# The 64 small transfers of the last attention are begun by GpSimd instead of SyncE

## The reference

```python
def first_block(x, ...):                 # gated linear attention + dilated attention, then a gated FFN
    x = x + mix @ w_out
    x = x + (silu(h2 @ w_gate) * (h2 @ w_up)) @ w_down

def second_block(x, ...):
    x = x + even_mixer(rms_norm_2(x), ...)   # retention and a short convolution
    x = x + odd_mixer(rms_norm_2(x), ...)    # the last attention

def odd_mixer(h, w_in, q_norm_w, k_norm_w, sinks, w_out, pos):
    q, k, v, gate = split(h @ w_in)          # 32 query heads, 4 key/value heads, 64 wide
    q = rope(rms_norm_2(q, q_norm_w), pos)
    k = rope(rms_norm_2(k, k_norm_w), pos)
    o = swa_sinks(q, k, v, sinks)            # softmax in a window of 128 tokens, with a sink per head
    return (o * silu(gate)) @ w_out
```

## Time and profile before

| | us |
|---|---|
| median of three runs (1873.78 to 1875.99) | 1874.39 |
| the profiled execution | 1875.87 |
| its span, first to last instruction | 1874.0 |
| TensorE busy in the span (99%) | 1862.7 |
| VectorE busy (66%) | 1246.1 |
| ScalarE busy (54%) | 1002.7 |
| GpSimd busy (2%) | 35.8 |

### The profile page before, as it was taken

How to read it: one execution, slowest core, us unless ns; L and a number is a source line. 1 busy time by engine, 2 the same in 40 slices (tenths; PEclk the granted TensorE clock), 3 DMA queues, 4 the chain that set the end, 5 groups by cost and what they waited for, 6 DMA issues and landing times.

```text
span 1874.0 us, 22288 instructions
## 1 busy us (share of the span) xinstructions
PE 1862.7 (99%) x8403; PEld 1534.2 (82%) x8403; DVE 1246.1 (66%) x1833; ACT 1002.7 (54%) x1422; POOL 35.8 (2%) x90
## 2 busy tenths in 40 slices
PE   9999999999999999999999999999999999999999
PEld 7888888888888888888888888888888888877777
DVE  6676566776666556665466776765676666776786
ACT  6677554554444344443444455564565545476763
POOL 0001000000000000000000000000000001001100
PEclk9999999999999999999999999999999999999999
DMA  9667764786666666666666686666666678677985
GB/s 324 202 194 179 207 183 151 215 257 192 195 193 193 193 191 191 193 197 196 189 198 194 201 281 203 192 191 190 185 203 198 193 238 241 202 234 216 268 255 174
DMA packets 223628, 388.36 MB, mean 207 GB/s; under 512 B 15696, under 2 KB 45184, under 8 KB 223520
## 3 DMA queue, kind: packets, MB, share of 16 engines
q1 hardware_dynamic: 222272, 384.17, 68.3%
q0 software_dynamic: 816, 2.11, 0.8%
q10 hardware_dynamic: 432, 0.66, 0.1%
HBM read 367.83 MB, written 19.05 MB: 206 GB/s over the span
## 4 chain that ended last, share of the span: by engine, by line
PE 95%; DMA 2%; DVE 1%; ACT 1%; SPq 0%; issue 0%; DVEq 0%; ACTq 0%
PE g L1341 31%; PE g L1342 30%; PE g L1343 30%; DMA PTB<-probs 1%; DMA queries<-TWQ 1%; DVE wl L1797 1%; PE ob L1404 1%; ACT wh L1513 0%; DMA queries<-TE 0%; DMA probs<-A 0%; PE m L1391 0%; PE m L1483 0%; DMA A<-queries 0%; PE m L1283 0%; DVE TWQ L1797 0%
## 5 line engine op out<-in xcount | busy, mean ns | idle before, releaser
L1797 DVE TENSOR_TENSOR wl<-raw,wh 128x1024 fp32r<-128x1024 f32 (+1 forms) x660 | 802.0, 1216 | 554.1 <-ACT wh L1513 551.0
L1513 ACT ACTIVATE wh<-raw 128x1024 fp32r<-128x1024 f32 (+1 forms) x661 | 695.2, 1053 | 750.2 <-PE g L1343 739.5
L1341 PE MATMUL g<-wh,xh 128*128 128x512 f32 x1886 | 740.7, 393 | 0.0
L1343 PE MATMUL g<-wh,xl 128*128 128x512 f32 x1886 | 735.6, 390 | 0.0
L1342 PE MATMUL g<-wl,xh 128*128 128x512 f32 x1886 | 735.6, 390 | 0.0
L1341 PEld LDWEIGHTS g<-wh,xh 128*128 128x128 f32 x1886 | 354.5, 188 | 78.4 <-issue 3.8
L1343 PEld LDWEIGHTS g<-wh,xl 128*128 128x128 f32 x1886 | 354.5, 188 | 74.1
L1342 PEld LDWEIGHTS g<-wl,xh 128*128 128x128 f32 x1886 | 354.6, 188 | 72.2
L1341 PE MATMUL g<-wh,mh 128*128 128x512 f32 x732 | 287.6, 393 | 0.4 <-issue 0.4
L1343 PE MATMUL g<-wh,ml 128*128 128x512 f32 x732 | 285.4, 390 | 0.0
L1342 PE MATMUL g<-wl,mh 128*128 128x512 f32 x732 | 285.3, 390 | 0.0
(11 more groups left out here) (175 smaller groups left out, 716.3 us busy)
## 6 DMA issues: line engine op xcount, KB each, us to landing
raw<-in_ev_w_in SPq DMA_DIRECT2D x128, 512.0 KB, 3.8
raw<-in_w_in SPq DMA_DIRECT2D x92, 512.0 KB, 4.4
raw<-in_w_gate SPq DMA_DIRECT2D x88, 512.0 KB, 4.4
raw<-in_w_up SPq DMA_DIRECT2D x88, 512.0 KB, 4.4
raw<-in_w_down SPq DMA_DIRECT2D x88, 512.0 KB, 4.8
raw<-in_od_w_in SPq DMA_DIRECT2D x72, 512.0 KB, 4.5
raw<-in_w_out SPq DMA_DIRECT2D x32, 512.0 KB, 4.2
raw<-in_ev_w_out SPq DMA_DIRECT2D x32, 512.0 KB, 4.8
```

The lines of the kernel that those rows point to most:

```text
L1341: e.matmul(o, hi[:, kt, c], h, start=first, stop=False)
L1343: last = e.matmul(o, lo[:, kt, c], h, start=False, stop=end)
L1513: return e.activation(o, i, AF.Copy, scale=scale)
L1797: return e.tensor_tensor(o, a, b, op)
```

## The change

SyncE no longer begins `qsend`, `qfetch`, `psend` and `pfetch`: the same 64 instructions with the same waits now stand in GpSimd's list, in the order of the plan. The plan's rules change with it: `on_root` is placed when the query fetch should have landed (so GpSimd's list has room for other transfers ahead of it), the assumed durations are 6 and 6.5 us for probabilities out and back (6.5 and 8.5 before) and 6.5 for the query fetch (7), `on_sum` is held until the transfer that reads its buffer has ended by 1.5 us, and VectorE may have a backlog of 4 us instead of 3 in the attention and 6 instead of 4.5 ahead of `mmul`. No computation changes.

```diff
@@ after(), queries @@
                     for i in range(2):
+                        while a[0] and self.end[("qsend", a[0] - 1, i)] + 1.5 > self.now:
+                            yield 1
                         say("on_sum", a[0], i)
@@ queries_back @@
             self.say("qfetch", j)
-            self.end[("qfetch", j)] = self.now + 7
-            yield 2
+            self.end[("qfetch", j)] = self.now + 6.5
+            while self.end[("qfetch", j)] > self.now:
+                yield 1
             self.say("on_root", j)
@@ probs_back @@
-        self.end[("psend", g)] = self.now + 6.5
+        self.end[("psend", g)] = self.now + 6
...
-        self.end[("pfetch", g)] = self.now + 8.5
+        self.end[("pfetch", g)] = self.now + 6.5
@@ fetched @@
-            yield from self.room("dve", 4.5)
+            yield from self.room("dve", 6)
             self.say("mmul", p[4])
@@ od_quad, five places @@
-            yield from self.room("dve", 3)
+            yield from self.room("dve", 4)
@@ gpsimd(): these four branches are taken out of sync() and stand here unchanged @@
+                elif kind == "qsend":
...
+                    e.dma_start(queries_there[k], queries_own[k]).then_inc(s_qsend[k], 16)
+                elif kind == "qfetch":
...
+                elif kind == "psend":
...
+                elif kind == "pfetch":
```

More of the change, by code:

```diff
@@ L587, in od_quad @@
             if (all(self.end.get(p, 1e9) <= self.now for p in [("qfetch", g // 2)] + self.ring[-3:][:2]) and
-                    self.through["dve"] - self.now <= 3):
+                    self.through["dve"] - self.now <= 4):
                 break
@@ L2351, in gpsimd @@
                     e.tensor_tensor(rsq[a[0]], py_, pq_, ALU.mult).then_inc(s_qroot, 1)
+                elif kind == "qsend":
+                    j, k = a
+                    on.wait_ge(s_qturn, 2 * j + k + 1)
+                    on.wait_ge(s_on_sum, nth("on_sum", j, k))
+                    if j:
+                        on.wait_ge(s_qback, 64 * j)
+                    e.dma_start(queries_there[k], queries_own[k]).then_inc(s_qsend[k], 16)
+                elif kind == "qfetch":
+                    j = a[0]
+                    for k in range(2):
+                        on.wait_ge(s_qsend[k], 16 * (j + 1))
+                    on.wait_ge(s_sent, sents[last_sent("xsent", "X3")])
+                    if j >= 2:
+                        on.wait_ge(*full("oqk", 2 * (j - 2) + 1, 1))
+                        on.wait_ge(s_qroot, j - 1)
+                    for i in range(4):
+                        e.dma_start(qo[32 * i:32 * i + 32, j % 2].rearrange("p k c n -> p (k c) n"),
+                                    t["queries"].rearrange("(a x) w -> x a w", a=8)[:, :, 130 * i:130 * i + 130]
+                                    ).then_inc(s_qback, 16)
+                elif kind == "psend":
+                    g = a[0]
+                    on.wait_ge(s_pturn, 2 * g + 2)
+                    if g >= 2:
+                        on.wait_ge(s_pback[g % 2], 64 * (g // 2))
+                    n = 18 if g % 2 else 15
+                    e.dma_start(probs_there[g % 2][:, 0:64 * n], A2[:, 1024:1024 + 64 * n]).then_inc(s_psend[g % 2], 16)
+                elif kind == "pfetch":
+                    g = a[0]
+                    on.wait_ge(s_psend[g % 2], 16 * (g // 2 + 1))
+                    on.wait_ge(s_pzero, 1)
+                    if g >= 2:
+                        on.wait_ge(s_pv, opened[("oapv", g - 2)])
+                    for i, (lo, hi) in enumerate(TURNED[g % 2]):
+                        at = 64 * (3 + g % 2) * i
+                        e.dma_start(probs_turned[g % 2][32 * i:32 * i + 32, :, 64 * lo:64 * hi],
+                                    probs_there[g % 2].rearrange("(m x) w -> x m w", m=4)[:, :, at + 64 * lo:at + 64 * hi]
+                                    ).then_inc(s_pback[g % 2], 16)
                 elif kind == "dec":
@@ L2430, in sync @@
                     e.dma_start(to, memory[n % 4].rearrange("p (i n) -> p i n", i=4)).then_inc(s_fetch[n % 4], 16)
[L2431 to L2467, removed]
                 elif kind == "out":
```

## The result

The changed kernel takes 1881.5 us (1877.7 to 1884.0, 13 runs) against 1874.4 us before; the ratio is 1.0037, interval 1.0030 to 1.0044. The prediction was 1868.9 us with a range from 1865.2 to 1876.0, and was wrong in sign. The profiled execution spans 1880.5 us, 6.5 more than before.

A forecast was written before the change was run, and what follows sets the result against it. TensorE, busy 99%, was taken as the bound, with 9.0 us of fetch waits and slow clock recoverable; less 3.5 of new waits, the 5.5 gain took 1875.87 to 1870.4, and the runs' median, 1.48 lower, to 1868.9 us (range 1865.2 to 1876).

The forecast's parts named there:

- The issues and the waits behind roots: GpSimd's list: 0.54 us per issue; behind roots of 5.8 us, `oapv` 1, 5 and 2 wait 0.4, 0.4 and 1.4.
- the third rival: GpSimd's issues wait for VectorE's `wl`, 0.9 us more on some 6 of 10: 1889 us, slower; chance 0.12.
- Queries, the step that failed: Before `oqk` 0, 2, 4, 6: fetched queries land 1.1 to 1.7 us ahead, so 1.2 us of waiting goes.
- 11.6 us: Query leg from `qturn` to data: second issue 0.54, send 4.4 and fetch 6.7 us on GpSimd's queue.
- the other end: Upper end for moved transfers, SyncE's durations: 6.2 us for `psend`, 5.5 for a query send, 7.2 for a fetch.
- the rival that followed it: Moved transfers take the same durations as SyncE's: 1873.9 to 1876.8 us, no change; chance 0.18.
- The clock: TensorE's clock in the last attention: no new wait is near 3.25 us, so 2.9 us of slow clock return.
- VectorE and ScalarE: In the last attention: more backlog allowed makes `wl` late, 1.0 us together; three other close places get nothing.
- The sum: Whole kernel: new waits 3.2 plus 0.3 for small ones make 3.5 us, against 9.0 returned: gain 5.5 us.

The follow-up runs named there:

- with 9.5: The changed kernel with the planner taking a query fetch as 9.5 us and a probability fetch as 7.5 (both 6.5 in the change): 1877.5 us.
- with 12 us: The changed kernel with the planner taking a query fetch to land 12 us after its start in place of 6.5: 1882.2 us.
- the move alone: The kernel before, with its order and planner numbers kept, and all query and probability transfers begun by GpSimd: 1890.3 us.
- roots behind: The kernel before with all these transfers begun by GpSimd, and in GpSimd's list roots 1 and 3 behind probability fetches 1 and 3: 1868.8 us.

## Why the prediction was wrong

- *The issues and the waits behind roots*: right in kind. An issue takes 0.54 to 0.62 us (0.54 forecast), so the third rival, issues held by VectorE, is out. Roots took 4.1 to 5.7 us against 5.8 taken. For probabilities I counted 2.2 us of new waits, 1.4 of them at `oapv` 2; 0.3 came, at `oapv` 1. That is partly luck: a fetch of probabilities took 5.1 to 10.3 us against 6.7 counted, and the data of group 0 were there 0.3 us before its `oapv`, on a TensorE that had just waited 1.7 us for queries.
- *Queries, the step that failed*: "11.6 us" from the second issue of a send to the fetched data, of which "a fetch of four parts 3 issues and the landing of the part behind another, 3 x 0.54 + 5.1 = 6.7". Measured for that fetch: 9.6 to 10.6, and for the whole leg 13.4 to 15.7 us. The distances, forecast at 12.7 to 13.3, were nearly right, 0.9 too long at block 3: from the end of the second `qturn` of blocks 0 to 3 the data took 16.0, 14.6, 13.7 and 14.1 us, and TensorE was ready after 13.4, 12.9, 14.5 and 12.0; what is missing are the three waits. Nor was it the send: 4.4 counted, 5.5 measured at block 0 and 3.1 to 3.5 at the others. No row of before had the fetch's burst on GpSimd's queue beside loads of weights; I put four parts at the price of one and took 7.2 for the other end. Both ends were too low. (SyncE's 7.2 was built on the row of `PTB<-probs`, 5.5 a part; the queries' own row of before has 4.0.) The runs put in their place: 4.8 and 5.2 us with little or nothing beside it, 9.6 to 10.6 beside the weights of the changed kernel. I weighed the rule that engines share the DMA engines, and then set it aside for one row of 4.7 us, a single transfer and not a burst; the rival that followed it gave 1873.9 to 1876.8 and was nearer, but its times for a fetch were too low as well.
- *The clock*: "none is near the 3.25 that the clock fell after". Behind waits of 2.71 and 2.19 us the granted clock was 0.61 and 0.60 on average, 3.4 us that the sum had at nothing.
- *VectorE and ScalarE*: the mechanism (more backlog allowed, `wl` late) was right, the size was not: 1.0 us counted at units 600 and 637 (0.4 and 0.6), 4.7 measured in six waits. These two units had 0.2 and 1.4; units 636 and 624, at which the sum had 1.1 us to spare and nothing, had 0.8 and 1.7. At the longest one, unit 624, ScalarE runs the exponentials of a group back to back ahead of `wh`, and VectorE's `wl` follows it (ScalarE's timeline):

```profile
1754.10 0.43 ACT L1659 ACTIVATE A<-A,st 128x64 f32<-128x64 f32 x1
...
1757.87 1.04 ACT L1516 ACTIVATE wh<-raw 128x1024 fp32r<-128x1024 f32 x1
```

  `wh` waited 13.5 us for weights between 1600 and 1850 us where it was 3.4 before, but none of these waits ends within 7 us ahead of one for `wl`. The run with the old allowances takes 2.9 us of the `wl` waits away; whether the rest comes from the slipped scores or from the order itself was not separated.
- *The sum*: 9.0 back, 3.5 lost was forecast. Measured: the same 9.0 are replaced by 15.0, 6.6 + 3.4 of them with the queries and 4.7 with `wl`; 0.5 us of the span's 6.5 is not placed.

## What to carry to other kernels

A transfer that is moved off the list of an engine with a steady stream of loads no longer stands between them, but it still shares the DMA engines with that stream, and some of the loads land later as well: measure or bound the landing in a burst beside the stream, not from a lone transfer. On the queue that takes it over, ask for each entry what stands ahead of it and for what that waits; here two roots ahead of two fetches were worth 21 us, and putting them behind turned the move into the fastest version. An order that is tightened to a hoped-for duration leaves nothing for an error: three of four fetches became waits here. Loosening that one number afterwards only moved the wait; what paid was the move on the old, looser order, so make the move first, look at the landings, and tighten then.

## What the runs showed of the hardware

- The same four parts of a fetch (520 KB) on GpSimd's queue landed in 4.8 us with nothing and in 5.2 with little beside them, in 5.8 and 6.8 beside two or three loads of weights alone (third fetches of the runs with 9.5 and with 12 us), and in 9.6 to 10.6 beside the loads and other small transfers of the changed kernel; on ScalarE's queue in 9.3 to 13.9. On the weights' own queue it was 4.5 to 8.6 before, and 5.4 to 11.8 in the run with the fetch alone on SyncE.
- The slowest loads of weights took longer too: at most 8.4 us in the last attention before the change, 10.8 after it and 11.5 in the run with 12 us.
- Sends of 260 KB took 2.6 and 3.3 us (medians) on GpSimd's queue in the changed kernel, where the earlier trace rows have 5.5 on SyncE's. On the same queue, but in the order of before, they took 4.5 and 4.9 (the move alone) and 5.5 (roots behind), so the queue by itself is not shown to be faster. The sends of probabilities, of 480 and 576 KB, went from 5.9 and 6.2 to 5.5 and 5.9.
- GpSimd's small instructions of a root, 0.22 us each, took up to 1.33 in the move alone, so that one root lasted 8 us.
